# Dealing the rows of a gather and scatter over blocks of eight partitions, in a hybrid-attention and expert layer

## The chip, the cores and the metric

One core of one Trainium2 chip runs the whole kernel. The metric is the device time of one execution, in microseconds. The engines are TensorE (PE: matmuls; PEld: its weight loads), VectorE (DVE), ScalarE (ACT), GpSimd (POOL), SyncE (SP: issues the plain DMAs), and the core's 16 DMA engines.

## The reference, cut to what matters

The layer normalises its input, runs three kinds of attention, adds the result, and passes it to a mixture of experts in two levels. 512 tokens of width 2048 choose one of 8 groups, and in it 2 of 8 experts. Each expert has three matrices of 2048 x 256. All of it is in float32.

```python
g_prob = softmax((xt @ wg) + bg)                 # 8 groups
g_p, g_idx = lax.top_k(g_prob, 1)
e_in = take_along_axis(e_logits, g_idx)          # the 8 experts of that group
e_val, e_loc = lax.top_k(e_in, 2)
weight = g_p * softmax(e_val)
y[token] += weight * ((silu(xc @ w_gate[e]) * (xc @ w_up[e])) @ w_down[e])
out = rms_norm(x + y, ln_f)
```

## The kernel before, in words

**Attention (to about 950 us).** Projections, attention and the output projection are tiled in 128 tokens. The result, the rows before the experts, is stored to a DRAM scratch of 512 rows of 8 KB (`x2_dram`). The change does not touch this part, except that a table of constants is loaded in it (line 692).

**Routing (about 967 to 988 us).** VectorE makes a one-hot of each token's group. TensorE counts with it (lines 1233 to 1240), and `grank` (line 2122) is the rank of a token among those of its group, from 0. Line 2123 compares `row_iota` with `grank`: `row_hot[token, p]` is 1 where partition p is the token's row. A matmul with `row_hot` (`place_rows`, line 1203) turns this into `idx_i[p, g]`, the token that partition p holds for group g, or 4096, out of range, where it holds none (line 2130). Before the change `row_iota` is 0 to 127, so that rank r is in partition r.

**Gather and scatter.** On POOL, `gather` (line 855) copies the column of one group to `g_idx` and reads those rows of `x2_dram` into `xg[b]`, one row of 8 KB into one partition; `scatter` (line 867) writes them to the output. Both are indirect DMAs over 128 partitions, and an index out of range moves no row. The order is written out in `pool_pass` (line 875): gather 0; gather 1 once three experts are through; then for each group g its scatter, and the gather of g + 2, which waits for that scatter (line 858), since both use the same of two buffers.

**The experts (about 988 to 1940 us).** The groups run in turn, and in each its 8 experts. A matmul with `pick` copies an expert's rows, up to 64, out of `xg` into slots (`pick_half`, line 1256, twice per group). `gate_up` (line 1329) multiplies them with the gate and up matrices, `down_product` (line 1366) with the down matrix, and `spread_result` (line 1311) adds the 64 results to the rows of the group: `spread[slot, p]` is 1 where partition p holds the slot's token (line 2216, again with `row_iota`). After a group the sums are added to `xg`, normalised (`last_norm`, line 2237) and scattered.

**The weights.** SP loads them in the order of `LOAD_ORDER` (line 237), 192 matrices of 2 MB in eight slots (`load_chunk`, line 727; loop at line 793). A load waits until PE has used what was in its slot (`chunk_used`, line 745), so that there are up to seven or eight loads ahead. Each spans 128 partitions of 16 KB. `gate_up` waits for its two loads at the semaphores of line 1306. For the first group the loop waits for the first gather (line 784) before it goes on.

**The end.** SP waits until all eight scatters have landed (line 837). A branch for groups over 128 rows or experts over 64 is not taken with this input.

Of the kernel before, what the change touches and what calls it, by code (L numbers as in the profile page):

```python
# [17 lines left out]
P = 128  # L18
# [36 lines left out]
MISC = FOX_HEADS + 3 * NSA_HEADS  # L55


C_IDENT = 0
C_TRI = C_IDENT + P
TRI_W = T + 3 * P  # L60
# [3 lines left out]
C_CANY = C_CMASK + NT * CMP_PAD  # L64
C_DIAG = C_CANY + NT
C_IOTA = C_DIAG + P
C_TOK = C_IOTA + P
C_ROWS = C_TOK + NT
C_ALL = C_ROWS + P
N_SMALLS = 12  # L70
# [144 lines left out]
        SPLITS[step, 1].append((ALL_TILES + a, part))  # L215


CAP = 64
PASSES = T // CAP
PER = PER_GROUP  # L220
SLOTS = 6
# [2 lines left out]
FAST_SLOTS = SLOTS + 2  # L224
HALF = PER // 2 * CAP
BANK_ORDER = (0, 2, 1, 3)
# [4 lines left out]
def last_user(turn, j):  # L231

    return max((i for i in range(j) if turn[i] == turn[j]), default=None)
assert 2 * CAP == P and CHUNKS % SLOTS == 0 and PER % 2 == 0

# [32 lines left out]
def constants():  # L268

    c = np.zeros((P, C_ALL), np.float32)  # L270
    p = np.arange(P)
    c[:, C_IDENT:C_IDENT + P] = np.eye(P, dtype=np.float32)
    c[:, C_TRI:C_TRI + TRI_W] = p[:, None] <= np.arange(TRI_W)[None, :] - 3 * P


    rel = 2 * P - 1 - np.arange(STRIP)
    half = BUCKETS // 2
    n = np.maximum(rel, 0)
    nf = np.maximum(n, half).astype(np.float32)
    large = half + (np.log(nf / np.float32(half)) / np.float32(math.log(MAX_DISTANCE / half))  # L280
                    * np.float32(BUCKETS - half)).astype(np.int32)
    bucket = np.where(n < half, n, np.minimum(large, BUCKETS - 1))
    strip = np.zeros((BUCKETS + 1, STRIP), np.float32)
    seen = rel >= 0
    strip[bucket[seen], np.arange(STRIP)[seen]] += 1.0
    strip[BUCKETS - 1, seen] -= 1.0
    strip[BUCKETS, ~seen] = 1.0
    c[:BUCKETS + 1, C_BUCKET:C_BUCKET + STRIP] = strip
    t = np.arange(T).reshape(NT, P)
    end = CMP_STRIDE * np.arange(CMP_PAD) + CMP_BLOCK - 1  # L290
    valid = (end[None, None, :] <= t[:, :, None]) & (np.arange(CMP_PAD) < N_CMP)
    c[:, C_CMASK:C_CANY] = np.where(valid, 0.0, NEG).transpose(1, 0, 2).reshape(P, -1)
    c[:, C_CANY:C_DIAG] = valid.any(-1).T
    c[:, C_DIAG:C_IOTA] = np.where(p[None, :] <= p[:, None], 0.0, NEG)
    c[:, C_IOTA:C_TOK] = np.arange(P)
    c[:, C_TOK:C_ROWS] = t.T
    c[:, C_ROWS:] = np.where(np.arange(P) < CAP, np.arange(P), -5000.0)
    return c


# [48 lines left out]
def hybrid_block_moe_kernel(nc, x_in, ln1, w_in, diff_lambda, diff_subln, fox_bf, cmp_pos_k, cmp_w1_k,  # L349
# [3 lines left out]
    with ExitStack() as ctx:  # L353
        def sb(name, shape, dt=F32):
            return ctx.enter_context(nc.sbuf_tensor(name, shape, dt))
# [21 lines left out]
        def region(at, *shape, memory=arena):  # L377
            n = int(np.prod(shape))
            (a, whole), = [(a, t) for (a, b), t in memory.items() if a <= at and at + n <= b]
            flat = whole[:, at - a:at - a + n]  # L380
            if len(shape) == 1:
                return flat
            names = "abcd"[:len(shape)]
            return flat.rearrange(f"p ({' '.join(names)}) -> p {' '.join(names)}",
                                  **{k: v for k, v in zip(names[1:], shape[1:])})
# [38 lines left out]
        y_high = region(RING0 + 24 * KB, 2, T, memory=rounded)  # L424
        pick = region(RING0 + 28 * KB, PER * CAP)
        silu = region(RING0 + 30 * KB, D_EXPERT)
# [5 lines left out]
        consts = sb("consts", [P, C_ALL])  # L432
        ident = consts[:, C_IDENT:C_IDENT + P]
        tri = consts[:, C_TRI:C_TRI + TRI_W]
# [1 line left out]
        cmask = consts[:, C_CMASK:C_CANY].rearrange("p (q n) -> p q n", q=NT)  # L436
        diag = consts[:, C_DIAG:C_DIAG + P]
        iota = consts[:, C_IOTA:C_IOTA + E_ALL]
        row_iota = consts[:, C_IOTA:C_IOTA + P]
        cap_rows = consts[:, C_ROWS:C_ROWS + P]  # L440
        hidT = consts[:, C_TRI + 2 * P:C_TRI + 3 * P].rearrange("p (a b) -> p a b", a=2)
        slot_of_row = consts[:, C_TRI + 3 * P:C_TRI + 3 * P + E_ALL]
# [66 lines left out]
        row_hot = region(AT0, NT, P)  # L509
        slot_hot = region(AT0 + 2 * KB, 2, NT, CAP)  # L510
        y_low = region(AT0, 2, T, memory=rounded)
# [133 lines left out]
        def row_to_all(ap, offset, n):  # L645

            return bass.AP(ap.tensor, offset, [[0, P], [1, n]])
# [5 lines left out]
        def _(sp):  # L653
# [29 lines left out]
            for t in range(NT):  # L683
                sp.dma_start(x_first[:, t, :], x_rows[:, t, :]).then_inc(x_in_sem[t], 16)
                if t == 0:
                    sp.dma_start(ln1_row, row_to_all(ln1, 0, D)).then_inc(ln1_in, 16)
                    sp.dma_start(ident, table[:, C_IDENT:C_IDENT + P]).then_inc(ident_in, 16)
                if t == 1:
# [1099 lines left out]
        def _(dve):  # L1788
# [38 lines left out]
            link(v.tensor_scalar(revi[:], iota, -1.0, float(E_ALL), ALU.mult, ALU.add))  # L1827
            link(v.tensor_scalar(tok_m[:], consts[:, C_TOK:C_ROWS], -float(OUT_OF_RANGE), None, ALU.add))
            v.tensor_copy(ones_b[:], ones)
# [512 lines left out]
```

## Time and profile before

| | us |
|---|---|
| median of 3 runs (1960.18 to 1960.65) | 1960.5 |
| the profiled execution, whole | 1959.72 |
| its span, first to last instruction | 1957.9 |
| PE busy | 1871.3 |
| DVE busy | 706.1 |
| ACT busy | 585.2 |
| POOL busy | 245.4 |
| DMA, plain queue, mean over the 16 engines | 66.2% |
| DMA, indirect queue (16 transfers, 8.39 MB), mean | 1.1% |

The profile is of one execution. Busy time is the time in which an engine ran at least one instruction; PE's is modelled, as its matmuls overlap. "L1352" is line 1352 of the kernel. The DMA rate is the sum over 16 engines. A wait is put down to what ended it last. The indirect transfers are q0, the plain ones q1.

### The profile page before, as it was taken

What the parts mean: (1) busy time and instruction counts of PE and PEld (TensorE: products, weight loads), DVE (VectorE), ACT (ScalarE), POOL (GpSimd) and SP (SyncE); (2) the same over time, 40 slices, a digit from 0 to 9 for tenths busy, and PEclk for the clock granted to TensorE, in tenths of its full rate; (3) what the DMA queues carried; (4) which work ended last, traced back from release to release, by engine and by line L of the source; (5) the groups of instructions that cost most, each with busy time, mean ns of one, the idle gap of its engine ahead of it and who ended that gap; (6) DMA issues with size and microseconds to landing.
All of it is one profiled execution on the core that took longest, in us unless ns stands there. A gap on an engine that the chain in (4) does not pass through costs nothing.

```text
span 1957.9 us, 28614 instructions
## 1 busy us (share of the span) xinstructions
PE 1871.3 (96%) x11946; PEld 1354.0 (69%) x11946; DVE 706.1 (36%) x1768; ACT 585.2 (30%) x1212; POOL 245.4 (13%) x208
## 2 busy tenths in 40 slices
PE   6999999999999999999999999989989899899996
PEld 5887777777777767788986666556566566655653
DVE  5331223333766668701142232313223123231322
ACT  5323333333544544322312232313113132131312
POOL 2433343333000000144100000000000000000000
PEclk9999999999999999999999999999999999999999
DMA  9554233233322331155589999999999999999994
GB/s 279 138 147 115 70 81 86 65 81 82 62 58 44 74 127 48 44 172 184 213 353 413 427 426 427 428 427 427 426 428 426 427 424 428 425 418 428 420 423 163
DMA packets 177394, 505.92 MB, mean 258 GB/s; under 512 B 52835, under 2 KB 136163, under 8 KB 151147
## 3 DMA queue, kind: packets, MB, share of 16 engines
q1 hardware_dynamic: 174954, 495.63, 66.2%
q0 software_dynamic: 2304, 8.39, 1.1%
q8 instruction: 97, 1.59, 0.3%
q14 instruction: 39, 0.31, 0.0%
HBM read 495.85 MB, written 16.53 MB: 262 GB/s over the span
## 4 chain that ended last, share of the span: by engine, by line
PE 79%; DMA 18%; ACT 1%; DVE 1%; issue 0%; SPq 0%; POOL 0%; POOLq 0%; ACTq 0%; DVEq 0%
PE banks L944 25%; PE banks L1352 12%; DMA at_region<-in_w_up 9%; PE banks L1101 9%; DMA x_region<-in_w_up 8%; PE banks L1377 7%; PE banks L1274 6%; PE banks L1353 3%; PE banks L1081 3%; PE banks L1053 2%; PE banks L1031 2%; PE banks L1323 2%; PE banks L993 1%; PE banks L1192 1%; PE banks L1038 1%; PE banks L1362 1%
## 5 line engine op out<-in xcount | busy, mean ns | idle before, releaser
L944 PE MATMUL banks<-ht_rounded,ring_rounded 128*128 128x512 f32 x1056 | 359.3, 394 | 0.7 <-ACT at_region L1515 0.7
L944 PEld LDWEIGHTS banks<-ht_rounded,ring_rounded 128*128 128x128 f32 x1056 | 195.1, 188 | 53.4 <-issue 13.8
L1352 PE MATMUL banks<-at_region,ht_region 128*64 128x256 f32 x800 | 180.7, 385 | 14.7 <-DMA at_region<-in_w_up 14.7
L848 POOL TENSOR_TENSOR ring_rounded<-ring_region,at_rounded 128x512 fp32r<-128x512 f32 (+1 forms) x92 | 115.9, 1291 | 511.1 <-ACT at_rounded L1454 511.1
L1353 PE MATMUL banks<-at_region,ht_region 128*64 128x256 f32 x768 | 175.4, 388 | 0.0
L2234 DVE SCALAR_TENSOR_TENSOR at_rounded<-banks,small,ring_rounded 128x512 fp32r<-128x512 f32 x128 | 96.1, 750 | 208.5 <-ACT ring_rounded L1740 207.6
L2227 DVE COPY consts<-banks 128x128 f32<-128x128 f32 x64 | 18.7, 292 | 403.7 <-PE banks L1362 403.7
L1352 PEld LDWEIGHTS banks<-at_region,ht_region 128*64 128x64 f32 x800 | 109.8, 139 | 72.7 <-issue 26.8
L1740 ACT ACTIVATE ring_rounded<-banks,small 128x512 fp32r<-128x512 f32 x128 | 88.0, 687 | 240.1 <-PE banks L1377 240.1
L944 PE MATMUL banks<-ht_rounded,at_rounded 128*128 128x512 f32 x352 | 142.7, 405 | 1.0 <-ACT at_region L1507 0.7
L1730 ACT ACTIVATE ring_region<-banks,consts 64x256 f32<-64x256 f32 x64 | 30.1, 470 | 374.6 <-PE banks L1353 374.4
L944 PE MATMUL banks<-mix_rounded,at_rounded 128*128 128x512 f32 x352 | 137.6, 391 | 0.0
L944 PE MATMUL banks<-mix_rounded,ring_rounded 128*128 128x512 f32 x352 | 137.5, 391 | 0.0
L848 POOL TENSOR_TENSOR ring_rounded<-ring_region,ring_rounded 128x512 fp32r<-128x512 f32 x88 | 111.2, 1296 | 198.8 <-ACT ring_rounded L1454 198.8
L1101 PE MATMUL banks<-ring_rounded,ht_rounded 128*128 128x512 f32 x384 | 129.8, 392 | 0.0
L1274 PEld LDWEIGHTS banks<-ring_region,mix_region 128*128 128x128 f32 x512 | 116.7, 306 | 15.8 <-issue 12.2
L1274 PE MATMUL banks<-ring_region,mix_region 128*128 128x256 f32 x512 | 125.0, 399 | 0.0
L1352 PE MATMUL banks<-x_region,ht_region 128*64 128x256 f32 x480 | 111.2, 392 | 9.7 <-DMA x_region<-in_w_up 9.7
L1353 PE MATMUL banks<-x_region,ht_region 128*64 128x256 f32 x512 | 118.8, 392 | 0.0
L871 POOL DMA_INDIRECT out<-mix_region,g_idx x8 | 8.0, 1006 | 841.2 <-DVE mix_region L2244 841.2
L1353 PEld LDWEIGHTS banks<-at_region,ht_region 128*64 128x64 f32 x768 | 106.4, 140 | 0.0
L1352 PEld LDWEIGHTS banks<-x_region,ht_region 128*64 128x64 f32 x480 | 67.6, 142 | 49.8 <-issue 19.7
(297 smaller groups left out, 3483.6 us busy)
## 6 DMA issues: line engine op xcount, KB each, us to landing
at_region<-in_w_gate SPq DMA_DIRECT2D x24, 2048.0 KB, 29.6
at_region<-in_w_up SPq DMA_DIRECT2D x23, 2048.0 KB, 28.8
at_region<-in_w_down SPq DMA_DIRECT2D x22, 2048.0 KB, 24.2
ring_region<-in_w_in SPq DMA_DIRECT2D x36, 1024.0 KB, 6.0
x_region<-in_w_down SPq DMA_DIRECT2D x17, 2048.0 KB, 26.9
x_region<-in_w_up SPq DMA_DIRECT2D x15, 2048.0 KB, 30.0
x_region<-in_w_gate SPq DMA_DIRECT2D x14, 2048.0 KB, 30.8
ring_region<-in_w_gate SPq DMA_DIRECT2D x9, 2048.0 KB, 34.2
```

The source lines that it names most:

```text
L848: ins = nc.gpsimd.tensor_tensor(w_low[n % RING][:, ks, 0:width], ring[n % RING][:, ks, 0:width], w_high[n % 2][:, ks, 0:width].bitcast(F32 ...
L944: ins = mm(out, w[:, k, 0:width], h[:, k, :], start=k == 0 and i == 0, stop=k == KT - 1 and i == 2)
L1031: ins = mm(S[:, par, half, 0:W], q[pr][rows, cols], keys[kind == "win"][rows, 0:W], start=True, stop=True)
L1053: ins = nc.tensor.transpose(PT[:, half, kb * P:(kb + 1) * P], probs[:, n % 2, half, kb * P:(kb + 1) * P], ident)
L1081: ins = mm(o, v[:, kb, cols], pT[:, half, j * P:(j + 1) * P], start=kind == "fox" and kb == 0, stop=part != "slc" and kb == qb)
L1101: ins = mm(out, a[:, 4 * c + i, t * P:(t + 1) * P], b[:, i, :], start=first and i == 0 and k == 0, stop=last and i == 3 and k == 2)
L1274: mm(place[turn[j]][:, 0:HALF], rows[:, j, :], slots, start=True, stop=True).then_inc(picked, 1)
L1352: mm(place[0:CAP, 0:D_EXPERT], x, gate[j], start=j == 0, stop=j == KT - 1)
L1353: ins = mm(place[CAP:2 * CAP, 0:D_EXPERT], x, up[j], start=j == 0, stop=j == KT - 1)
L1377: ins = mm(PT[side * CAP:(side + 1) * CAP, m, :], hidT[:, j, :], down[:, j, (2 * side + m) * T:(2 * side + m + 1) * T], start=j == 0, stop ...
L1740: fn(y_high[:, m, :], PT[:, m, :], ACT.Copy, scale=own_weight[e8 % 2]).then_inc(y_a, 1)
L2234: v.scalar_tensor_tensor(y_low[:, m, :], PT[:, m, :], own_weight[e8 % 2], y_high[:, m, :].bitcast(F32), ALU.mult, ALU.subtract).then_inc(y ...
```

## The change

The column of the table that says which rank a partition holds is no longer 0 to 127 but a permutation of it: partition p holds rank (p mod 8) x 16 + floor(p / 8). So rank 0 is in partition 0, rank 1 in partition 8, rank 15 in partition 120, and rank 16 in partition 1. `row_hot` and `spread` are made with it. The comparisons with slots keep a column of their own, 0 to 63, and the table becomes 64 columns wider. Nothing else is edited.

```diff
+CAP = 64
...
 C_IOTA = C_DIAG + P
-C_TOK = C_IOTA + P
+C_RANK = C_IOTA + CAP
+C_TOK = C_RANK + P
 C_ROWS = C_TOK + NT
...
-CAP = 64
 PASSES = T // CAP
...
-    c[:, C_IOTA:C_TOK] = np.arange(P)
+    rank = np.arange(P) % 8 * (P // 8) + np.arange(P) // 8
+    c[:, C_IOTA:C_RANK] = np.arange(CAP)
+    c[:, C_RANK:C_TOK] = rank
     c[:, C_TOK:C_ROWS] = t.T
-    c[:, C_ROWS:] = np.where(np.arange(P) < CAP, np.arange(P), -5000.0)
+    c[:, C_ROWS:] = np.where(rank < CAP, rank, -5000.0)
...
         iota = consts[:, C_IOTA:C_IOTA + E_ALL]
-        row_iota = consts[:, C_IOTA:C_IOTA + P]
+        row_iota = consts[:, C_RANK:C_RANK + P]
```

## Rows read from the trace of the kernel before

**Rows 1.** The page, slices of the span: DMA busy share in tenths, rate.
```profile
DMA  9554233233322331155589999999999999999994
GB/s 279 138 147 115 70 81 86 65 81 82 62 58 44 74 127 48 44 172 184 213 353 413 427 426 427 428 427 427 426 428 426 427 424 428 425 418 428 420 423 163
```

**Rows 2.** Windows: length, busy times, PE's clock share, DMA share, GB/s.
```profile
1055.00:1060.00 5.00, 5.00 (x30) 2.15 (x30) 1.72 (x5) 1.22 (x3) 0.00 (x0) 1.00 0.81 308
...
1388.67:1510.73 122.06, 114.13 (x801) 74.26 (x801) 33.33 (x74) 28.11 (x52) 2.23 (x3) 0.99 1.01 427
```

**Rows 3.** Waits of PE from 1240 to 1950 us: total, times, longest.
```profile
PE banks L1352 <- DMA at_region<-in_w_up: 25.5, 12, 2.9
PE banks L1352 <- DMA ht_region<-in_w_up: 10.2, 5, 3.0
PE banks L1352 <- DMA x_region<-in_w_up: 9.7, 5, 2.6
```

**Rows 4.** The chain in order of time: start, length; PE resuming after an up weight.
```profile
1253.62 0.40 PE banks L1352
...
1376.60 0.40 PE banks L1352
...
1498.66 0.40 PE banks L1352
...
1621.90 0.40 PE banks L1352
...
1744.51 0.40 PE banks L1352
...
1865.68 0.40 PE banks L1352
```

**Rows 5.** Indirect queue, one short window around each gather, groups 0 to 7: packets, MB.
```profile
q0 software_dynamic: 144, 0.44, 28.9%
...
q0 software_dynamic: 144, 0.82, 25.1%
...
q0 software_dynamic: 144, 0.34, 10.3%
...
q0 software_dynamic: 144, 0.82, 20.1%
...
q0 software_dynamic: 144, 0.33, 9.3%
...
q0 software_dynamic: 144, 0.56, 14.4%
...
q0 software_dynamic: 144, 0.73, 18.6%
...
q0 software_dynamic: 144, 0.16, 5.5%
```

**Rows 6.** Windows of 0.31 us: two in the first gather, one in the last scatter.
```profile
985.13:985.44 0.31, 0.31 (x6) 0.31 (x5) 0.00 (x0) 0.00 (x0) 0.00 (x0) 1.00 0.37 159
...
985.75:986.06 0.31, 0.31 (x6) 0.31 (x4) 0.00 (x0) 0.00 (x0) 0.00 (x0) 1.00 0.31 132
...
1954.42:1954.73 0.31, 0.00 (x0) 0.00 (x0) 0.00 (x0) 0.00 (x0) 0.00 (x0) 0.50 0.37 132
```

**Rows 7.** DMA of the whole span: a queue (packets, MB), an issue (KB, us to landing).
```profile
q8 instruction: 97, 1.59, 0.3%
...
consts<-table SPq DMA_DIRECT2D x1, 900.0 KB, 9.4
```

**Rows 8.** Instructions around the first pick: start, length.
```profile
986.73 0.33 SPq L788 DMA_DIRECT2D mix_region<-in_w_up  x1
...
986.92 0.69 DVE L2147 TENSOR_TENSOR ring_region<-consts,small 128x512 f32<-128x512 f32 x1
...
987.67 7.53 PE L1274 MATMUL banks<-ring_region,mix_region 128*128 128x256 f32 x32
```

**Rows 9.** DMA issues after 1950 us.
```profile
out<-mix_region,g_idx POOLq DMA_INDIRECT x1, 4.6
```

## The prediction, made before the changed kernel was run

> **What bounds the kernel now.** I read the page's slices first, then the chain of waits, then the waits of TensorE (PE), and last the DMA queues in short windows. The slices (49 us each) show two halves [rows 1]: after the first, the DMA moves 44 to 213 GB/s up to about 980 us; from 1028 us on it moves 413 to 428 GB/s in every slice but the last. The change touches only the second half, the experts, where the 16 DMA engines are the full resource. PE is near it: a stretch of one group (eight experts, 24 loads of 2 MB) has PE busy for 114.1 of 122.1 us while the DMA moves 427 GB/s [rows 2]. From 1240 us on PE waits 45.4 us in 22 pieces (25.5 + 10.2 + 9.7), always for an up weight that is landing [rows 3]. So from the first such wait at 1253.62 us to the last loads the end is set by when weights land, and not by work on PE.
>
> **Landing means landing on the slowest engine**, and the rows say how slow it is. The chain resumes on the same kind of load once per group, at 1253.62, 1376.60, 1498.66, 1621.90 and 1744.51 [rows 4], so four groups take 490.89 us, 122.7 each. 24 loads are 50.33 MB; at 427 GB/s that is 117.9 us. One engine has 427/16 = 26.7 GB/s, so one row of 8,192 bytes costs it 0.307 us. With 8 rows of a scatter and 8 of a gather on the same engine: 117.9 + 16 x 0.307 = 122.8 us, which is what is measured. If rows were spread evenly, the 579 rows of those eight transfers (100+100, 42+40, 100+68, 40+89, by the sizes below) would cost every engine the same, and a group (50.33 MB + 145 x 8,192 B)/427 = 120.7 us. The difference, 2 us per group, is what balanced rows could give back. [...]
>
> **Group sizes** come from the megabytes of the indirect queue at each gather, divided by 8,192 B and rounded so that they sum to 512 [rows 5]: 54, 100, 42, 100, 40, 68, 89, 19 rows. The other descriptors of the 128 are out of range and carry 4 bytes.
>
> **Which engine serves which partition** decides everything, and the title of the change assumes an answer (eight neighbouring partitions are one engine). The first gather and the last scatter run with nothing beside them, and a slice of 0.31 us holds one row per working engine, 26.7 GB/s each [rows 6]. With 54 rows in partitions 0 to 53, neighbouring eights would keep six engines busy to the end (160 GB/s). The rate instead falls to 159 and ends on 132 GB/s: five engines. That fits groups of four partitions dealt in turn to eight engines, with partitions 32 to 63 dealt to the same eight again: loads of 8, 8, 8, 8, 8, 6, 4, 4. With 19 rows, eights would give three engines, 80 GB/s; the row shows 132, five engines (4, 4, 4, 4, 3). A third witness is the group with the small gather: from 1744.51 to 1865.68 us, 121.17 us [rows 4]; eights predict 16 rows and 122.8, fours predict 8 + 4 rows and 121.6. I take fours. Partitions 64 to 127 must be on the other eight engines: the stretch with two transfers of 100 rows (1253.62 to 1376.60, 122.98 us) leaves no room for the 32 rows, 127.7 us, that a single set of eight would get.
> [...]
>
> **The change, part by part.** (1) The table grows by 64 columns, 32 KB on a load of 900 KB at the start [rows 7]: 0.08 us at 427 GB/s, beside other loads; zero taken. (2) The two comparisons that read the rank columns keep their shapes: zero. No instruction, wait, DMA or queue is added, removed or moved; scatter and gather move the same rows. Matmuls contract over all 128 partitions as before. (3) What is left is the place of the rows. Rank r goes to partition 8(r mod 16) + floor(r/16). For the first 64 ranks the inner part is 0 to 3, so they fill every other group of four: in the map above that is engines 0, 2, 4, 6 and 8, 10, 12, 14, and none of the odd ones. Two blocks (b and b+4) share an engine. The odd engines come in only with rank 64. Before, 64 rows also sat on eight engines. So the busiest engine has, before and after, per group size: 54: 8, 8; 100: 8, 8; 42: 8, 6; 100: 8, 8; 40: 8, 6; 68: 8, 8; 89: 8, 8; 19: 4, 3.
> In the stretch where landing decides lie the scatters of groups 0 to 6 and the gathers of 2 to 7. Engine 0, the busiest, has 56 + 44 = 100 rows before and 52 + 39 = 91 after. **Nine rows x 0.307 = 2.8 us.** The gather of group 1 (1028 to 1036 us) is ahead of a dip to 308 GB/s [rows 2], where the queue ran dry because PE had not freed slots; what it saves is lost there (and it saves nothing, 8 against 8).
> (4) Instruction fetches are 97 packets of 16.4 KB over the span [rows 7], 0.61 us each, and a packet is on one engine. Before, two engines tie at 100 rows and the next has 88; after, four are at 91, 91, 90, 89, so a fetch finds a bound engine more often. How they fall on the engines no row shows. Bounds: one fetch fewer or one more on the slowest engine, -0.6 to +0.6 us; with more engines tied I take half of the upper one, 0.3 us lost.
> (5) The first gather: 8 rows on the busiest engine before and after; and SyncE goes on at 986.73 us, which shows the landing, while the pick table is ready only at 987.61 and the first pick starts at 987.67 [rows 8]. A gain would be hidden by up to 0.9 us of VectorE's work. Zero.
> (6) The last scatter is at the end of everything, 4.6 us from issue to landing [rows 9]: 4 rows to 3 on its busiest engine, 0.3 us.
> Sum: 2.8 - 0.3 + 0.3 = 2.8 us. The profiled execution took 1959.72 us (span 1957.9), so 1956.9; the median of the three runs is 0.8 us above it, which gives **1957.7 us**.
>
> **The rivals.** *Full balance.* If eights were engines after all, engine 0 would go from 104 rows to 61 in the stretch, 43 x 0.307 = 13.2 us, and the last scatter from 8 rows to 2, 1.8 us: 15.0 us, 1945.5 us. For it: the plan of the change, and the periods of 122.7 us, which both maps give. Against it: three readings above. Chance 0.08.
> *Nothing.* Nine rows are spread over 680 us, and the two smallest savings could vanish where engines that now tie with engine 0 lag by a fetch; then 0 to 0.5 us is left, 1960.2 us. For it: the tie of four. Against it: a lag of the slowest engine is paid in full in the periods of rows 4. Chance 0.20.
> *Slower.* The change now uses the upper 64 partitions in every transfer. If those were served by the same eight engines as the lower ones, groups of up to 64 rows would fall on four engines: the busiest would have 14, 16, 11, 16, 10, 16, 16, 5 rows instead of 8, 16, 8, 16, 8, 12, 12, 4, in the stretch 173 against 140, and 33 x 0.307 = 10.1 us gives 1970.6 us. It decides as soon as an upper partition shares an engine with an even lower group. Against it: the 122.98 us above, and 427 GB/s, which needs 16 engines. Chance 0.04.
>
> **How the numbers follow.** Forecast 0.68, with its own range of 1956.0 to 1959.5 us: a map that is right leaves one or two rows and 1 us of fetches open each way. Nothing 0.20, full balance 0.08, slower 0.04. A measurement of this kernel can tell about 0.2%, 3.9 us, from no change. Faster than that: all of full balance and a fifth of the forecast's case (1956.6 us lies near the lower end of its range), 0.22; slower 0.04; within it 0.74. The range leaves out full balance and the slower case: 1954.5 to 1961.0 us.
>
> **What would show it.** In the profile after, the last scatter's short slices should show eight engines at first (213 GB/s) and end sooner, where full balance would show sixteen; the first gather should again reach about 210 GB/s at most and last as long. The periods between the landings of rows 4 should be 122.8, 121.6, 122.8, 122.2, and 121.3 us in order; full balance would give about 122.2, 119.7, 121.6, 120.7 and 120.0. PE's waits for up weights should fall from 45 to about 42 us. Periods near 120 us, or a first gather at 400 GB/s, would prove my map wrong.

## The result: slower by 0.2%, and the profile after

Over 20 runs each, the changed kernel takes **1963.55 us** (1961.77 to 1966.88) and the kernel before 1959.49 us. The ratio is **1.0021, 95% interval 1.0015 to 1.0028**. The forecast was 1957.7 us with a range up to 1961.0, so the measured time is 5.9 us above the forecast and 2.6 us above the range. The 4.1 us between the two kernels are little, but the interval leaves no room for a gain. The profiled execution took 1964.48 us (span 1962.6, before 1957.9). Lines of the file have moved by three (L1355 is the L1352 of [rows 4]), and by a few more in some kernels of the experiments.

First, what TensorE waits for from 1240 us on (us in total, times, longest); it answers to [rows 3]:

```profile
PE banks L1355 <- DMA at_region<-in_w_up: 29.5, 12, 4.2
PE banks L1355 <- DMA x_region<-in_w_up: 9.8, 5, 2.6
PE banks L1355 <- DMA ht_region<-in_w_up: 2.1, 2, 1.4
```

With 1.2 us for a fourth buffer that is 42.6 us, where it was 45.4: less, as the step on rows said it would be, and yet the time has risen. The fall proves nothing, because TensorE itself was slower between the waits. In the stretch of one group it is busy for longer than in [rows 2] (114.13 us at a granted clock of 0.99), so less of the same lateness is left to wait for:

```profile
1388.67:1510.73 122.06, 115.90 (x804) 74.68 (x802) 33.34 (x74) 28.12 (x52) 2.22 (x3) 0.97 1.01 427
```

Also, the longest wait is now 4.2 us. The chain, by the piece in which the awaited load lands, once per group (start, length; TensorE resumes 0.14 us after its end), against [rows 4]:

```profile
1227.79 26.25 DMA at_region<-in_w_up
...
1351.25 26.68 DMA at_region<-in_w_up
...
1474.06 25.62 DMA at_region<-in_w_up
...
1596.25 27.26 DMA at_region<-in_w_up
...
1719.45 27.29 DMA at_region<-in_w_up
...
1842.95 24.23 DMA at_region<-in_w_up
...
1879.44 35.71 DMA at_region<-in_w_up
...
1915.28 0.66 PE banks L1355
```

The ends are 1254.04, 1377.93, 1499.69, 1623.51, 1746.74, 1867.18: periods of 123.9, 121.8, 123.8, 123.2 and 120.4 us. Before they were 123.0, 122.1, 123.2, 122.6 and 121.2. Those with large transfers got longer, though the busiest engine has no more rows in them. The final wait ends at 1915.28 us; in the trace of before it ended at 1912.70. That is 2.6 us of the 4.7 us between the spans.

The other part is TensorE's clock. The last three columns are its granted clock, the DMA share and GB/s. After the wait of 4.2 us it is granted about half of its full clock (0.52 and 0.63 in two windows of 4 us; the clock record has 0.50 for 6.8 us):

```profile
1912.00:1914.00 2.00, 0.00 (x0) 0.00 (x0) 0.65 (x1) 0.00 (x0) 0.00 (x0) 1.00 0.99 406
1914.00:1918.00 4.00, 2.72 (x14) 1.81 (x16) 0.00 (x0) 0.00 (x0) 0.00 (x0) 0.52 1.02 414
1918.00:1922.00 4.00, 4.00 (x26) 2.60 (x24) 0.00 (x0) 0.00 (x0) 0.00 (x0) 0.63 0.79 303
```

The trace of before has 1.00 in all three windows. From the end of the wait to the issue of the last scatter it takes 42.81 us (1915.28 to 1958.09) instead of 40.01 (1912.70 to 1952.71): 2.8 us. How the 4.7 us divide depends on the trace taken for the old placement. That of experiment 1 resumes at 1912.32 us, and its clock does drop behind the last wait, for about half as long; against it the change costs 3.0 us by the landing and 0.7 us behind it. The last scatter itself gives a little back (windows of 0.31 us, and its issue to landing; against [rows 6] and [rows 9]):

```profile
1959.13:1959.44 0.31, 0.00 (x0) 0.00 (x0) 0.00 (x0) 0.00 (x0) 0.00 (x0) 0.50 0.39 133
1959.44:1959.75 0.31, 0.00 (x0) 0.00 (x0) 0.00 (x0) 0.00 (x0) 0.00 (x0) 0.50 0.61 212
1959.75:1960.06 0.31, 0.00 (x0) 0.00 (x0) 0.00 (x0) 0.00 (x0) 0.00 (x0) 0.50 0.36 132
```

```profile
out<-mix_region,g_idx POOLq DMA_INDIRECT x1, 3.8
```

212 GB/s is eight engines of 26.7 GB/s, as forecast (213). Rows over all sixteen show more: the even placement of experiment 2 reaches 396 GB/s at this place. So the map by fours stands. Against the trace of before the sum is 2.6 + 2.8 - 0.7 = 4.7 us. The question is why weights land later although the busiest engine carries nine rows less.

**What the landing records say.** The trace notes when each sixteenth of a load arrives. The last of the sixteen is what TensorE waits for: before the final wait of the changed kernel they arrive from 1899.64 to 1915.15 us, 15.5 us apart, and TensorE resumes at 1915.28. Latest arrivals of neighbouring loads are 4.9 us apart in quiet stretches. In the changed kernel one gap near 1446 us is 6.42 us, and the DMA queues in the 5 us before it (1441 to 1446) show a single foreign packet:

```profile
q8 instruction: 1, 0.02, 1.3%
```

1.3% of 16 engines x 5 us is 1.04 us of one engine's time, and the load is 1.5 us late. The same happens at 1594, 1747 and 1905 us, behind every eighth of these packets, and in the second trace of the change (e7) at 1445, 1593, 1746 and 1905. In the trace of before the same line stands in 1435 to 1440 us, and the loads behind it keep their 4.9 us. The packet is code (`instruction`), in pieces of 16.4 KB about every 19 us. That it is TensorE's is inferred from the counts on the page: the 97 pieces are 67 bytes for each of its 23,892 instructions, but would be 899 for each of the 1,768 of the next engine, and the instructions added in experiment 3 brought 32 each. This is the term which the prediction put at 0.3 us in all. The theory tested below: **a code packet delays the engine it falls on by about 1.5 us, these packets fall on only half of the engines, and the change put its heavy sets of rows on some of those.** The rival is that rows alone count, and that the 4 us have another cause (the wider table, say). Engines are numbered by the prediction's map, 8 x (partition >> 6) + ((partition >> 2) & 7). That it holds in the upper 64 partitions too was the author's assumption; the even placement (e2) bears it out.

### The profile page after: what moved, and what is told of

Its sections match the earlier page's. It is cut to its first block, busy times and chain, and to the rows that moved or that the text cites. A ratio compares the mean times of both kernels' runs of the same rounds, so it can differ in the third digit from the quotient of the medians.

```text
span 1962.6 us, 28614 instructions
## 1 busy us (share of the span) xinstructions
PE 1879.2 (96%) x11946; PEld 1358.9 (69%) x11946; DVE 705.6 (36%) x1768; ACT 585.3 (30%) x1212; POOL 245.7 (13%) x208
## 3 DMA queue, kind: packets, MB, share of 16 engines
q8 instruction: 97, 1.59, 0.3%
## 4 chain that ended last, share of the span: by engine, by line
PE 78%; DMA 19%; ACT 1%; DVE 1%; issue 0%; SPq 0%; POOL 0%; POOLq 0%; ACTq 0%; DVEq 0%
PE banks L947 25%; PE banks L1355 12%; DMA at_region<-in_w_up 10%; PE banks L1104 9%; DMA x_region<-in_w_up 9%; PE banks L1380 7%; PE banks L1277 6%; PE banks L1356 3%; PE banks L1084 3%; PE banks L1056 2%; PE banks L1034 2%; PE banks L1326 2%; PE banks L996 1%; PE banks L1195 1%; PE banks L1041 1%; PE banks L1365 1%
## 5 line engine op out<-in xcount | busy, mean ns | idle before, releaser
L1355 PE MATMUL banks<-at_region,ht_region 128*64 128x256 f32 x800 | 183.4, 389 | 15.1 <-DMA at_region<-in_w_up 15.1
L1356 PE MATMUL banks<-at_region,ht_region 128*64 128x256 f32 x768 | 184.8, 403 | 0.0
L1355 PEld LDWEIGHTS banks<-at_region,ht_region 128*64 128x64 f32 x800 | 111.1, 140 | 75.6 <-issue 30.4
L1355 PE MATMUL banks<-x_region,ht_region 128*64 128x256 f32 x480 | 109.5, 388 | 11.5 <-DMA x_region<-in_w_up 10.3
L1356 PEld LDWEIGHTS banks<-at_region,ht_region 128*64 128x64 f32 x768 | 110.7, 146 | 0.0
L1355 PEld LDWEIGHTS banks<-x_region,ht_region 128*64 128x64 f32 x480 | 66.5, 140 | 49.0 <-issue 23.6
```

The costliest lines, as they stand in the source:

```text
L1355: mm(place[0:CAP, 0:D_EXPERT], x, gate[j], start=j == 0, stop=j == KT - 1)
L1356: ins = mm(place[CAP:2 * CAP, 0:D_EXPERT], x, up[j], start=j == 0, stop=j == KT - 1)
```

## The experiments

All kernels start from the changed one and alter only the line that sets `rank`, unless said. Ratios and differences are to runs of the kernel before made beside each (medians 1958.3 to 1959.7 us). "Rows" is the number of rows on the busiest engine in the stretch of the prediction.

**1. The old placement with the new table; the even placement; one that spares the suspected engines; the old one mirrored.**

```
e1:  rank = np.arange(P)
e2:  engine = 8 * (np.arange(P) // 64) + np.arange(P) // 4 % 8
     place = np.arange(P) % 4 + 4 * (np.arange(P) // 32 % 2)
     rank = 16 * place + engine
e3:  fetches = (engine >= 7) & (engine <= 14)
     rank = np.argsort(np.argsort((place + 2 * fetches) * 32 + 16 * fetches + engine))
e4:  rank = np.arange(P) ^ 64
```

> Rank r goes back to partition r, everything else of the change stays (the wider table, the second set of columns). Both theories: the place of the rows is all there is, so the time is that of the kernel before, ratio 1.000, within 1 us; rows on the busiest engine in the stretch where landing decides: 100. If the wider table or the second comparison costs what I put at zero, this stays at +4 us and the place of the rows is innocent. It is also a second trace of the old placement: if instruction fetches fall on engines in a pattern of their own, loads must again land late by about 1.5 us at the same fetches.

Measured 1959.2 us, ratio 1.0000 (0.9991 to 1.0009). The wider table and the second set of columns cost nothing within that interval; the 4 us come from the place of the rows. The delays of 1.5 us at single fetches that I expected here are not in this trace: from 1100 us on, away from gathers and scatters, the largest are two of 0.7 us.

> The placement that the map of fours asks for: one rank per engine in turn over all sixteen. Busiest engine in the stretch: 61 rows instead of 100 before and 91 after; last scatter 2 rows instead of 4. Rows alone: 39 x 0.307 = 12.0 us earlier, and 0.6 at the last scatter: 12.6 us below the kernel before, 1947. Rows and instruction fetches (theory: each costs the engine it falls on about 1.5 us, and they fall on eight engines only, 7 to 14 in my numbering, about 8.6 us each in the stretch): the slowest engine goes from 31.9 us of extra work to 25.2, 6.7 us less, with the last scatter 7.3: 1952. If neighbouring eights were engines instead, this placement would be no better than the one before.

Measured 1952.0 us, ratio 0.9959 (0.9945 to 0.9972): 7.7 us faster, where the two theories said 7.3 and 12.6. The map by fours is right: 16 of the 19 rows of the last scatter lie here in 16 different fours, eight of them in the upper partitions, and its first slice shows 396 GB/s, 14.8 engines of 26.7. Rows alone promise too much.

> Like the placement by fours, but the engines 7 to 14 get two rows fewer per transfer and the others more: 74 rows at most on engines outside 7 to 14, 39 inside. Rows alone: 74 rows cost 22.7 us, 4.0 us more than the placement by fours, so it is 4.0 us slower than that one (1951). Rows and fetches: slowest engine 22.7 us of extra work against 25.2 with fours and 31.9 before, so 2.5 us faster than fours and 9.2 us below the kernel before, 1950. Which of the two is faster tells the theories apart, whatever the size.

Measured 1956.4 us, ratio 0.9986 (0.9977 to 0.9995). 4.4 us slower than the even placement: this is what rows alone forecast, and **a miss for my theory as it stood**. Either it is wrong, or its list of engines is.

> The placement before, mirrored: rank r in partition r xor 64, so the same row counts sit on engines 8 to 15 instead of 0 to 7 (100 at most). Rows alone: no difference to the kernel before, ratio 1.000. Rows and fetches: engine 8, 9 and 10 have 100, 100 and 88 rows and the fetches too, 30.7 + 8.6 = 39.3 us against 31.9 before: 7.4 us slower, ratio 1.004, and loads land late by about 1.5 us at nearly every fetch.

Measured 1965.6 us, ratio 1.0030 (1.0019 to 1.0042). Rows alone allow no difference here, since the row counts are only exchanged between the halves: 5.9 us are there. So something other than rows loads the engines unequally, and the upper ones more.

**2. The list of engines.** No record names a packet's engine. The landing records constrain it: for a list, each engine's row counts and its packets give sixteen arrival times per load, to be compared with those noted. I fitted the eight engines of the cycle (the packets repeat in their durations with a period of eight) to the traces at hand, and tested the list by new placements. e5 and e6 deal the same row counts in another order of engines:

```
role = np.argsort(ORDER)[engine]
rank = 64 * (role // 8) + 4 * (role % 8) + np.arange(P) % 4 + 32 * (np.arange(P) // 32 % 2)
e5:  ORDER = [0, 1, 2, 3, 7, 8, 14, 15, 4, 5, 6, 9, 10, 11, 12, 13]
e6:  ORDER = [4, 5, 6, 9, 10, 11, 12, 13, 0, 1, 2, 3, 7, 8, 14, 15]
e9:  ORDER = [0, 1, 2, 3, 6, 8, 13, 15, 4, 5, 7, 9, 10, 11, 12, 14]
e10: fetches = np.isin(engine, [4, 5, 7, 9, 10, 11, 12, 14])     (else as e3)
```

> The row counts of the kernel before (100, 100, 88, 84, 83, 78, 76, 76 and down to 12), dealt to other engines: the eight heavy sets go to engines 0, 1, 2, 3, 7, 8, 14, 15. Rows alone: the busiest engine has 100 rows as before, ratio 1.000. Rows and fetches with my first list of fetched engines (7 to 14): engine 14 has 76 rows and the fetches, engine 8 has 78: 24.3 + 8.4 = 32.4 us against 31.9, no change. Rows and fetches with the list that fits the landings of the five placements seen so far (engines 4, 5, 6, 9, 10, 11, 12, 13, about 1.5 us a fetch, 8.4 us each): the slowest engine is then a fetch-free one with 30.7 us against 33.9 before, 3.2 us faster, 1956.4, ratio 0.9984.

Measured 1959.8 us, ratio 0.9999 (0.9990 to 1.0008): no gain. If the theory holds, the list has a fetched engine among its free ones.

> The mirror of the run with the heavy sets on engines 0, 1, 2, 3, 7, 8, 14, 15: the same row counts, the eight heavy sets on the eight engines that the fit calls fetched (4, 5, 6, 9, 10, 11, 12, 13). Rows alone: ratio 1.000 again, and no difference between the two. Rows and fetches by the fitted list: the busiest engine has 100 rows and the fetches, 30.7 + 8.4 = 39.1 us against 33.9 before: 5.2 us slower, 1964.9, ratio 1.0027, and 8.4 us above its mirror. If the list is wrong the two lie close together.

Measured 1965.6 us, ratio 1.0030 (1.0017 to 1.0042): 6.1 us slower, 5.8 us above its mirror with the same row counts. Rows alone are refuted again.

> The changed kernel once more, for a second trace. If the 6.8 us at half TensorE clock after the last stall (from 1914.4 us) belong to the placement, they and the stall of 4.2 us are there again and the span is about 1962.6. If they were a chance of that one execution, the clock in 1914 to 1922 us is full and the span is about 2.6 us shorter, while the loads land as late as before.

Measured span 1962.1 us. The clock drop is there again, after a wait of 4.2 us:

```profile
1912.00:1914.00 2.00, 0.00 (x0) 0.00 (x0) 0.00 (x0) 0.00 (x0) 0.00 (x0) 0.86 1.01 414
1914.00:1918.00 4.00, 3.53 (x18) 2.30 (x20) 0.00 (x0) 0.00 (x0) 0.00 (x0) 0.50 0.96 390
1918.00:1922.00 4.00, 4.00 (x30) 2.72 (x28) 0.00 (x0) 0.00 (x0) 0.00 (x0) 0.71 0.76 291
```

> The row counts of the kernel before once more, the eight heavy sets now on engines 0, 1, 2, 3, 6, 8, 13, 15. A fit to the landings of all nine traces so far calls engines 4, 5, 7, 9, 10, 11, 12, 14 the fetched ones (it explains the latest landing of each load within about 1 us in every one of them, and why the run with heavy sets on 7 and 14 gained nothing). Rows alone: ratio 1.000. Rows and fetches with this list: slowest engine 30.7 us against 33.9, 3.2 us faster, 1956.3, ratio 0.9984. If the list is still wrong in one heavy engine: about 0.

Measured 1961.6 us, ratio 1.0011 (1.0002 to 1.0020). A miss.

> One rank per engine in turn, with two rows fewer per transfer on the engines 4, 5, 7, 9, 10, 11, 12, 14 (35 to 39 rows) and more on the others (67 to 74). Rows alone: 74 rows, 4 us slower than the even placement, 1956. Rows and fetches with this list: slowest engine 22.7 us against 27 with the even placement and 33.9 before, 11 us faster than before at the loads; with 3 rows for 4 at the last scatter 1948, ratio 0.994, and 3 to 4 us faster than the even placement. If one of the engines with 74 rows is fetched after all: 31 us, 1956.

Measured 1956.1 us, ratio 0.9982 (0.9973 to 0.9991): the number given there for a list still wrong in one heavy engine. Each of the three lists has missed at least once. The theory needed a test that does not hang on the whole list.

**3. More code, and nothing else.** GpSimd does little in this half besides the gathers and scatters. After the scatter of each of the groups 0 to 6, and the gather that follows it, it now passes 1024 waits on a count reached long ago:

```
e8:  rank = np.arange(P)
     ...
+                    if isinstance(c, int) and g < N_GROUPS - 1:
+                        for _ in range(1024):
+                            pool.wait_ge(x2_stored, 16 * NT)
```

> The placement of before (rank r in partition r), with 7 x 1024 instructions more on GpSimd, which has nothing to do there: waits on a count that was reached long ago, after each scatter and gather. [...] Rows alone, or fetches at no cost: ratio 1.000. Fetches cost the engine that they fall on: if these go to the same eight engines as the others, 28/8 x 1.5 = 5.2 us slower; if they are spread over all sixteen, or come in packets of half the size, 1 to 3 us slower; if they fall on engines with slack alone, nothing.

Measured 1974.6 us, ratio **1.0075** (1.0062 to 1.0089): 15.2 us slower, three times the most that I had expected, and I had put only 1 to 3 us for packets of half the size, which is how they came. The DMA queues of the whole span: queue 8 is unchanged, queue 14 has 66 packets, where the run with the same placement and no added code has 38.

```profile
q8 instruction: 97, 1.59, 0.3%
q14 instruction: 66, 0.54, 0.1%
```

28 packets of 8 KB are 0.23 MB beside 506, 32 bytes for each of the 7,168 added instructions. The 28 in the expected 5.2 us is the count that came (66 against 38), but no run shows 16.4 KB to a packet for GpSimd's code. The latest arrivals of loads, from the landing records of both runs, with added packets at 1295.3, 1306.4 and 1318.0 us (and one that both have, at 1316.5 us in the run with added code):

```
placement of before:   1288.3 1293.2 1298.1 1303.0 1307.9 1312.8 1317.7 1322.6   gaps 4.9 throughout
with added code:       1289.7 1294.6 1300.1 1305.0 1310.5 1315.4 1321.0 1325.9   gaps 4.9, but 5.5 at 1300.1, 1310.5, 1321.0
```

Each added packet makes the next load land 0.6 us later, and nothing gives it back. That is what would be seen if all of them fell on one engine that is, or becomes, the slowest. In the trace with added code the last awaited load comes at

```profile
1887.82 36.41 DMA at_region<-in_w_up
1924.37 0.40 PE banks L1358
```

12 us after that of the run without it (1912.32). The spans of the two profiled executions differ by 12.0 us too; the 3 us more between the medians stand in no trace.

**4. The same code, fewer rows under it.** If the packets cost only the engine they fall on, then taking the rows off that engine must make the added code free. e11 exchanges the rows of engines 7 and 15, e14 those of engines 2 and 15.

```
e11: rank = np.where(p // 4 % 8 == 7, p ^ 64, p)
e14: ORDER = [0, 1, 15, 3, 4, 5, 6, 7, 8, 9, 10, 11, 12, 13, 14, 2]
```

> The 7 x 1024 idle instructions on GpSimd again (27 more code packets of 8 KB on queue 14, which cost 15 us with the placement of before, 0.65 us each at the latest landing), now with the rows of engine 7 and engine 15 exchanged: engine 7 has 12 rows instead of 76. Theory: all packets of queue 14 fall on engine 7, which then has 3.7 us of rows + 5.9 of queue 14 as before + 17.6 of the added code = 27.2 us, below the 33 us of the slowest engine, so the same ballast costs nothing: 1959.4, ratio 1.000. Rival: the code packets cost whatever the rows do (they are spread, or they hold up GpSimd): again 15 us, ratio 1.0075. If they fall on another engine than 7: also about 15 us.

Measured 1974.8 us, ratio 1.0077 (1.0063 to 1.0091): all 15 us still there, so it is not engine 7. A fit that gives GpSimd's packets an engine of their own put them on engine 2, with 0.5 us of error at the latest arrivals of both runs; the other small packets go best on engine 3, and TensorE's on 5, 6 and 9 to 14.

> The added GpSimd code once more, now with the rows of engine 2 exchanged with those of engine 15 (engine 2 has 12 rows in the stretch instead of 88). Theory: GpSimd's code packets all fall on engine 2 (a fit to both runs with the added code puts them there and leaves 0.5 us of error at the latest landing; the exchange of engines 7 and 15 did not touch it). Engine 2 then has 3.7 us of rows and 17.6 of added code, below the 33 us of the slowest engine: no cost, 1959.4, ratio 1.000. Rival: the added code costs 15 us wherever the rows are, ratio 1.0075, because it holds up GpSimd or because its packets are spread.

Measured **1959.7 us, ratio 1.0005 (0.9995 to 1.0014)**. The code is fetched as in e8 (97 packets on queue 8 and 66 on queue 14), and TensorE resumes after the last long wait at 1911.89 us instead of 1924.37:

```profile
1879.04 32.71 DMA at_region<-in_w_up
1911.89 0.40 PE banks L1360
```

Same instructions, same packets, same rows in all: 15 us, or nothing within the interval, by whether one DMA engine has 88 or 12 rows. This shows that GpSimd's code packets take their time from the one engine they fall on, and rules out that the added waits held up GpSimd. For TensorE's packets no such exchange was made.

**5. A placement by the refitted list.** One row fewer per transfer on engines 5, 6 and 9 to 14; e12 has a tie break on engine 7, e15 on engine 3; e13 repeats e2.

```
place = place + np.isin(engine, [5, 6, 9, 10, 11, 12, 13, 14]) + 0.5 * (engine == 7)   (e15: engine == 3)
rank = np.argsort(np.argsort(64 * place + engine))
```

> One rank per engine in turn, with one row fewer per transfer on engines 5, 6, 9, 10, 11, 12, 13, 14 (41 to 48 rows in the stretch) and, as a tie break, on engine 7 (54), against 61 to 65 on the others. The list is from a fit to the landings of all twelve traces, with queue 14 on engine 7. Rows alone: 65 rows, 1 us slower than the even placement, 1953. Rows and code: slowest engine 23.7 us against 25.9 for the even placement and 32.9 before; with 2 rows for 4 at the last scatter 9.8 us below the kernel before, 1949.6, ratio 0.995, 2 us below the even placement. If one of the engines with 61 to 65 rows is fetched after all: 28 us, 1954.

Measured 1950.3 us, ratio **0.9954** (0.9941 to 0.9968), 8.5 us faster.

> The even placement once more, on the chip of the run that shifts one row off the fetched engines, so that the two can be compared: 1952, ratio 0.996 as before; a second trace must have its loads land 7 us earlier than before.

Measured 1952.7 us, ratio 0.9965 (0.9952 to 0.9979), 6.1 us faster.

> As the placement with one row fewer on engines 5, 6, 9 to 14, with the tie break on engine 3 instead of engine 7: by the last fit the ten small code packets of queue 14 in the stretch fall on engine 3, 6.5 us. Slowest engine 23.7 us against 25.2 with the tie break on 7, 25.9 with the even placement and 32.9 before. Expected 9.8 us below the kernel before (1949.6, ratio 0.995), about 1.5 us below the run with the tie break on 7, which differs by less than the two can be told apart.

Measured 1950.1 us, ratio 0.9956 (0.9942 to 0.9970), 8.2 us faster. The 1.5 us that the other tie break should gain over e12 are not there, in the time or in the landings, so engine 3 as the place of the small packets is not borne out. e12 and e15 beat both kernels, by 8 us the one before and by more than 12 the changed one. Forecast were 9.8 us for each. Their intervals overlap that of the even placement, so the last 2 us between these and that one are likely but not settled. The last scatter of e15 takes 3.5 us from issue to landing.

**All runs beside one sum.** The sum is rows x 0.307 + 9.0 us on engines 5, 6, 9 to 14 (45 fetches in the stretch, 5.6 each at 1.6 us) + 6.5 on engine 3 (ten small packets) + 17.6 on engine 2 with the added code (27 x 0.65). Shown are the differences to the kernel before, in us: rows alone, the sum of the slowest engine, how much later the last 28 loads land in the trace (mean), and the median time.

```
                      rows alone   sum     landed   time
e1  old placement         0         0       0.0     -0.5
    the change           -2.8     +3.4     +2.1     +4.1
e7  the change again     -2.8     +3.4     +1.0     +4.4 (one run)
e2  even                -12.0     -7.1     -6.9     -7.7
e13 even again          -12.0     -7.1     -7.5     -6.1
e3  spares 7 to 14       -8.0     -3.1     -3.7     -3.3
e10 second list          -8.0     -3.1     -2.7     -3.3
e12 refitted list       -10.7     -7.7     -8.1     -8.5
e15 refitted list       -10.7     -9.2     -7.1     -8.2
e4  mirrored              0       +6.8     +6.7     +5.9
e6  heavy on fetched      0       +6.8     +6.5     +6.1
e5  heavy on first list   0       -0.6     +0.9     +0.3
e9  heavy on second       0       +1.5     +0.5     +2.2
e8  added code            0      +11.7    +10.6    +15.2
e11 added code, 7<->15    0      +11.7    +10.9    +16.0
e14 added code, 2<->15    0         0      -0.5     +1.4
```

The sum is within 2.4 us of the landings everywhere, rows alone are off by up to 11. The list was fitted on the traces up to e13, so only e14 and e15 test it as it stands: e14 bears it out (0 and -0.5), and e15 lands 2.1 us later than its sum.

## Why the prediction was wrong

**Step (4), the instruction fetches, failed, by its size and by its engines.** It took 0.61 us a packet, which is what a weight packet of the same size takes in the trace; the code packets are noted at 1.06. The page had the better price: [rows 7] give 97 packets 0.3% of 16 engines' span, 0.3% x 1957.9 x 16 / 97 = 0.97 us each, and I read only the count and the megabytes. The landing is later still, by about 1.5 us a packet. And I wrote that how they fall on the engines no row shows, and then took the effect of one packet, 0.3 us. Over the stretch it is 45 packets, by the fitted list on eight engines, 9 us on each of these and none on the rest: as much as 29 rows. With that, the busiest engine before is not engine 0 with 100 rows (30.7 us) but engine 5 with 78 rows and the fetches (32.9), and after the change engine 6 has 89 rows and the fetches (36.3). A balance of rows was computed on engines that were not the bound. Small packets of 8 KB were not counted at all. The rival *Nothing* had the right idea in its tie of four engines that lag by a fetch, but let it take away the gain and no more.

**Step (3), the place of rows,** was right as far as it went. Transfers of about 40 rows got shorter: the period with 42 and 40 rows fell by 0.3 us (forecast 0.5). The map by fours and the two halves of eight engines hold: the last scatter shows 212 GB/s where eight engines were forecast, and the even placement, made from that map, is 6 to 8 us faster. The rival of full balance under the title's map (0.08) is out.

**Steps (1), (2)** cost nothing: e1 at 1.0000. **Step (5)** stands: the pick table is ready at 987.05 us and the first pick starts at 987.11, still after SyncE has gone on (985.99). **Step (6)** gave 0.8 us (4.6 to 3.8) for 0.3.

**The slower rival** (upper partitions on the lower engines) is wrong in its mechanism, though its sign came true: the upper partitions are served by other engines, but these, by the fitted list, carry most of TensorE's code (e4, with the rows on them, is 5.9 us slower). A slower case by fetches belonged beside it; the text had noted four tied engines and stopped there.

**The clock** was not in the prediction. It adds time: the last wait, late by landing, also grew longer (1.7 us before, 4.2 after), and TensorE starts after it at half its full clock (0.50 in the record). The runs bear this out: the 38 runs of the kernel before with a mean clock of 0.992 or more took 1958.8 us on average, the 15 with 0.989 or less 1960.4; of the 20 runs of the changed kernel 13 are at 0.989 or less (1964.0). At like clocks the two kernels differ by 3.2 us (only two runs of the changed one at 0.992) to 3.6 us, so the landings are probably the larger part and the clock about 1 us. In the 17 traces the time from the last long wait to the end is 44.2 to 45.2 us where the clock stays full behind it (six traces), 45.4 to 46.7 where it drops for 3.4 us (nine), and 47.3 and 47.6 in the two traces of the change, where it drops for 6.8 us. The length of the wait alone does not decide: 3.0 us in e2 is followed by no drop, 2.0 us in e12 by the short one, and 4.2 us in e9 and e11 by the short one too. Why the change gets the long one stays open.

**Open.** The list of TensorE's engines comes from a fit and could be wrong in one that never carried many rows. Why a packet noted at 1.06 us (or 0.31 for the small ones) costs 1.5 (0.65) was not tried.

## What to carry to other kernels

Where the DMA engines are the full resource, as here at 427 GB/s and a share of 1.01, a load lands when its slowest engine is done (its sixteenths arrived up to 15.5 us apart before the final wait): add up per engine everything that falls on it, the kernel's own code included, before balancing one of the terms. A queue of 1.59 MB with 0.3% in the page decided here, by the fit because its packets are not spread evenly: divide its share by its packets first. To find out whether a small transfer costs anything, add more of it, then take the other work off the engine it falls on; the two runs together say more than any fit.

## What the runs showed of the hardware that was not expected

- A code packet of 16.4 KB (TensorE's, as inferred above) is noted at 1.06 us on average and delays the landing of the load by about 1.5 us where it falls on the slowest engine, while a packet of 16 KB of weights takes 0.61 (median of the 23,552 in the trace); an 8 KB packet of queue 14 is noted at 0.31 and delays by 0.62 to 0.66.
- 1024 instructions more for each of seven groups on a nearly idle engine, 0.23 MB in all, cost 15.2 us out of 1959, because all of their code comes over one DMA engine that was nearly the slowest; on an engine with few rows they cost nothing (1.0005, 0.9995 to 1.0014).
- The same row counts on other engines are worth from 0.3 to 6.1 us (e5 against e6).
